# The routing stage of a fused encoder block: tiles signalled singly, bf16 counts, a shorter chain of small operations, batched one-hot tables, and a gather straight from the table

## The reference

```python
mixed = (g_attn * (attn @ w_branch_attn) + g_rnn * (rnn @ w_branch_rnn)) @ w_out
x = x + gate_m * _rmsnorm(mixed, g_post_mix)
h = _rmsnorm(x, g_pre_ffn) * (1 + scale_f) + shift_f
logits = h @ w_router + b_router
top_val, top_idx = lax.top_k(logits, 4)
top_w = softmax(top_val)
# every token goes to its 4 experts; an expert works on blocks of at most 128 rows
y[t] = sum_k top_w[t, k] * expert[top_idx[t, k]](h[t])
x = x + gate_f * _rmsnorm(y, g_post_ffn)
```

## Time and profile before

| | us |
|---|---|
| median of 3 timed runs | 1868.07 (1867.8 to 1868.69) |
| the profiled execution's own time | 1865.61 |
| its span in the profile | 1863.9 |
| PE busy in the span | 1677.9 (90%) |
| DVE, ACT, POOL busy | 1386.0, 1048.5, 303.3 |

### The profile page before, as it was taken

The page is one execution under the profiler, slowest core; times in us unless marked ns, Lnnn a source line. Parts: engine busy times, 40 slices in busy tenths (PEclk is TensorE's granted clock), DMA queues, the critical chain, the costliest instruction groups (busy, mean ns, idle before and its releaser), DMA issues.

```text
span 1863.9 us, 21055 instructions
## 1 busy us (share of the span) xinstructions
PE 1677.9 (90%) x6959; PEld 1241.7 (67%) x6959; DVE 1386.0 (74%) x1228; ACT 1048.5 (56%) x1037; POOL 303.3 (16%) x282
## 2 busy tenths in 40 slices
PE   1899999988897568999999999999999999999872
PEld 1667678876676556777767777777776777777640
DVE  5778755765553757888898898898889889888626
ACT  2246732455521315776687677677667757766511
POOL 0400000100000010231321322223142132322010
PEclk9899999998999569999999999999999999999985
DMA  8434145221136337999999999999999999999535
GB/s 316 131 136 136 51 143 202 93 72 46 46 135 224 147 142 287 392 400 392 406 407 388 389 418 384 383 412 393 378 401 399 382 378 415 380 375 404 203 143 227
DMA packets 113857, 519.83 MB, mean 279 GB/s; under 512 B 17555, under 2 KB 50675, under 8 KB 59507
## 3 DMA queue, kind: packets, MB, share of 16 engines
q1 hardware_dynamic: 98970, 491.34, 67.3%
q0 software_dynamic: 9568, 17.23, 2.7%
q10 hardware_dynamic: 5272, 10.67, 1.6%
HBM read 514.46 MB, written 19.66 MB: 287 GB/s over the span
## 4 chain that ended last, share of the span: by engine, by line
PE 63%; DVE 15%; issue 9%; ACT 8%; DMA 3%; SPq 1%; POOL 0%; DVEq 0%; POOLq 0%; ACTq 0%
PE ps L2064 28%; PE ps L2080 13%; PE ps L1797 9%; DVE lo L1649 7%; PE ps L1982 2%; PE ps L1997 2%; PE ps L2036 2%; ACT hi L1075 2%; ACT hi L846 1%; DMA xt<-x_dram 1%; PE ps L2051 1%; PE ps L1864 1%; PE ps L1911 1%; PE ps L2044 1%; DVE gmin L1682 1%
## 5 line engine op out<-in xcount | busy, mean ns | idle before, releaser
L1649 DVE TENSOR_TENSOR lo<-raw,hi 128x2048 fp32r<-128x2048 f32 x318 | 716.7, 2286 | 155.0 <-ACT hi L1075 155.0
L1075 ACT ACTIVATE hi<-raw 128x2048 fp32r<-128x2048 f32 x318 | 596.8, 1911 | 231.3 <-PE ps L2064 217.0
L1797 PE MATMUL ps<-hT,hi 128*128 128x512 f32 x720 | 240.6, 409 | 15.9 <-DVE qbd L1416 8.1
L2064 PE MATMUL ps<-hi,x_a 128*128 128x512 f32 x864 | 243.0, 411 | 0.0
L742 POOL TENSOR_TENSOR ticks<-eps 128x1 f32<-128x1 f32 x100 | 78.5, 785 | 740.6 <-ACT ysb L1112 716.2
L2064 PEld LDWEIGHTS ps<-hi,x_a 128*128 128x128 f32 x864 | 162.3, 191 | 42.3 <-issue 9.4
L1797 PEld LDWEIGHTS ps<-hT,hi 128*128 128x128 f32 x720 | 138.7, 193 | 54.6 <-issue 15.9
L1797 PE MATMUL ps<-hT,lo 128*128 128x512 f32 x360 | 142.9, 397 | 0.0
L2064 PE MATMUL ps<-hi,x_b 128*128 128x512 f32 x480 | 137.1, 407 | 3.9 <-DVE lo L1649 2.8
L2080 PE MATMUL ps<-raw,a 128*128 128x512 f32 x288 | 129.4, 592 | 0.0
L2064 PE MATMUL ps<-raw,x 128*128 128x512 f32 x288 | 129.4, 592 | 0.0
(11 more groups left out here) (325 smaller groups left out, 2510.0 us busy)
## 6 DMA issues: line engine op xcount, KB each, us to landing
raw<-w_e_dram SPq DMA_DIRECT2D x396, 1024.0 KB, 8.8
raw<-w_ada_dram SPq DMA_DIRECT2D x24, 1024.0 KB, 6.8
raw<-w_in_dram SPq DMA_DIRECT2D x15, 1024.0 KB, 5.6
raw<-w_merge_gate_dram SPq DMA_DIRECT2D x8, 1024.0 KB, 5.3
yk<-yk_d SPq DMA_DIRECT2D x4, 2048.0 KB, 14.5
raw<-w_branch_rnn_dram SPq DMA_DIRECT2D x8, 640.0 KB, 4.8
raw<-w_branch_attn_dram SPq DMA_DIRECT2D x4, 1024.0 KB, 5.0
raw<-w_out_dram SPq DMA_DIRECT2D x4, 1024.0 KB, 4.8
```

What stands on the lines that cost most here:

```text
L1075: s.activation(hi[u.slot(i)][:, :], raw[i][:, :], ACT.Copy).then_inc(hi_done, 1)
L1649: v.tensor_tensor(lo[i][:, :], raw[i][:, :], hi[u.slot(i)][:, :].bitcast(F32), ALU.subtract).then_inc(split_done, 1)
L1797: last = mm(ps[:, bank, :], wk[:, k, c0:c0 + P], acts[xa][:, k0 + k, :], start=start and k == 0 and q == 0, stop=stop and k == kn - 1 and ...
L2064: last = mm(ps[:, q, :], x_, w[:, q * 512:(q + 1) * 512], start=False, stop=i == M1 - 1, skip_group_check=True)
```

## The change

It touches the routing stage alone.

- The last matmul of each of the first three tiles now raises a semaphore of its own, `op_ps`; ACT's `post_norm` waits for its own tile, and the fourth tile keeps the old wait.
- `hfT` becomes two buffers used in turn.
- `mask` is written as bf16 (`mask16`, with a fifth block of zeros), and the counts are made by bf16 matmuls: one of 160 columns against the triangle, then 10 of 32 columns against ones; the fifth block of columns is the count. All lie in one PSUM bank.
- The chain on DVE reads ranks and counts in place, does the overflow test for ranks and counts in one instruction of 160 columns, leaves out the copy and one memset (`iota_k` is prepared beforehand), and orders independent instructions so that each second one goes without a wait. The product with `oh` is one instruction of 512 columns instead of four of 128.
- The one-hot tables are made in two halves of 8 groups with three instructions each, in the type fp32r; PE waits once for each half.
- POOL zeroes `xg` before it waits for the table (it now also waits for the transfer of `x2`), and gathers by the table's first column itself.
- Buffers move (`oh_slot`, `pairs`, `prod`), and the table gets one more column. DVE has 5 more small instructions beside the output projection.

```diff
@@ tiles
+        hfT = [z(f"hfT{i}", [P, KT, P], F32, kb) for i, kb in enumerate((88, 106))]
-        oh_slot = z("oh_slot", [P, TOPK * TT, P], F32, 64)
-        oh_blk = z("oh_blk", [P, TOPK * TT, 64], F32, 72)
+        oh_slot = z("oh_slot", [P, TOPK * TT, P], F32R, 118)
+        oh_blk = z("oh_blk", [P, TOPK * TT, 64], F32R, 72)
+        mask16 = z("mask16", [P, TT + 1, NE], BF16, 117.5)
@@ gpsimd
-            pool.wait_ge(tab_done, 1)
             for i in range(TT):
                 pool.wait_ge(h2_out[i], 16)
+            pool.wait_ge(x2_out, 16)
             g.memset(xg[:, :], 0.0).then_inc(xg_zero, 1)
             pool.wait_ge(xg_zero, 1)
+            pool.wait_ge(tab_done, 1)
...
-            g.tensor_copy(idx_now[:, 0:1], tok_i[:, 0:1]).then_inc(idx_done, 1)
-            pool.wait_ge(idx_done, 1)
-            gather_dma()
+            gather_dma(tok_i[:, 0:1])
@@ scalar
-            act.wait_ge(chunk_used, W_MIX)
...
             def post_norm(i):
+                if i < TT - 1:
+                    act.wait_ge(op_ps, i + 1)
+                else:
+                    act.wait_ge(chunk_used, W_MIX)
...
-                if i:
-                    act.wait_ge(lg_ps, i)
-                s.activation(hfT[:, :, :], ...
+                if i >= 2:
+                    act.wait_ge(lg_ps, i - 1)
+                s.activation(hfT[i % 2][:, :, :], ...
@@ vector
+            v.tensor_copy(ahead16[:, :], before[:, :])
+            v.tensor_copy(ones16[:, :], ones[:, :])
+            link(v.tensor_copy(iota_k[:, :], iota_f[:, 0:NE]))
+            v.memset(iota_k[:, 0:1], -1e6)
+            link(v.memset(mask16[:, TT, :], 0.0))
...
-            link(v.tensor_copy(cnt, ps[:, 1, 0:NE]))
-            link(v.scalar_tensor_tensor(out=key, in0=cnt, scalar=float(NE), in1=iota_e, op0=ALU.mult, op1=ALU.subtract))
-            link(v.memset(key[:, 0:1], 1e6))
+            ranks = ps[:, 0, 0:(TT + 1) * NE].rearrange("p (i e) -> p i e", e=NE)
+            rank, cnt = ranks[:, 0:TT, :], ranks[:, TT, :]
+            link(v.scalar_tensor_tensor(out=key, in0=cnt, scalar=float(NE), in1=iota_k[:, :], op0=ALU.mult, op1=ALU.subtract))
...
+            link(v.tensor_scalar(q1, q0, 0.0, None, ALU.is_ge))
+            link(v.scalar_tensor_tensor(out=q1, in0=q0, scalar=float(P), in1=q1, op0=ALU.is_ge, op1=ALU.add))
+            v.tensor_scalar(pos, pos, -1.0, 0.0, ALU.add, ALU.max)
+            link(v.scalar_tensor_tensor(out=q1, in0=q0, scalar=float(2 * P), in1=q1, op0=ALU.is_ge, op1=ALU.add))
...
-            for t, val in ((0, blk), (1, q0)):
-                for k in range(TOPK):
-                    ins = v.tensor_tensor(prod[:, TT * k:TT * k + TT, :], oh[:, TT * k:TT * k + TT, :], val, ALU.mult)
-                link(ins)
+            for t, val in ((0, blk), (1, mask)):
+                link(v.tensor_tensor(prod4, oh4, val.unsqueeze(1).to_broadcast([P, TOPK, TT, NE]), ALU.mult))
                 link(v.tensor_reduce(pick[:, t, :], prod[:, :, :], AX_X, ALU.add))
...
             dve.wait_ge(x2_out, 16)
-            for q in range(TOPK * TT):
-                v.tensor_scalar(oh_slot[:, q, :], iota_f[:, :], pick[:, 1, q:q + 1], None, ALU.is_equal)
-                v.tensor_scalar(oh_blk[:, q, 0:N_TAB], iota_f[:, 0:N_TAB], pick[:, 0, q:q + 1],
-                                asgv[:, q // TT, q % TT:q % TT + 1], ALU.is_equal, ALU.mult).then_inc(oh_done, 1)
+            half = TOPK * TT // 2
+            for q in range(0, TOPK * TT, half):
+                n = slice(q, q + half)
+                link(v.tensor_tensor(oh_blk[:, n, 0:N_TAB], iota_f[:, 0:N_TAB]..., pick[:, 0, n]..., ALU.is_equal))
+                v.tensor_tensor(oh_slot[:, n, :], iota_f[:, :]..., pick[:, 1, n]..., ALU.is_equal).then_inc(oh_done, 1)
+                v.tensor_tensor(oh_blk[:, n, 0:N_TAB], oh_blk[:, n, 0:N_TAB].bitcast(F32), asgv..., ALU.mult).then_inc(oh_done, 1)
@@ tensor
+                    if q == 3 and i < TT - 1:
+                        last.then_inc(op_ps, 1)
                 last.then_inc(chunk_used, 1)
...
-            for i in range(TT):
-                for j in range(i + 1):
-                    mm(ps[:, 0, i * NE:(i + 1) * NE], before[:, :] if j == i else ones[:, :], mask[:, j, :], ...)
-            for i in range(TT):
-                last = mm(ps[:, 1, 0:NE], ones[:, :], mask[:, i, :], start=i == 0, stop=i == TT - 1)
+            mm(ps[:, 0, 0:(TT + 1) * NE], ahead16[:, :], mask16[:, :, :]..., start=True, stop=False, ...)
+            for j in range(TT):
+                for i in range(j + 1, TT + 1):
+                    last = mm(ps[:, 0, i * NE:(i + 1) * NE], ones16[:, :], mask16[:, j, :], start=False, stop=j == TT - 1, ...)
...
             for q in range(TOPK * TT):
-                pe.wait_ge(oh_done, q + 1)
+                if q % (TOPK * TT // 2) == 0:
+                    pe.wait_ge(oh_done, 2 + 2 * (q // (TOPK * TT // 2)))
                 last = mm(ps[:, 2, 0:N_TAB], oh_slot[:, q, :], oh_blk[:, q, 0:N_TAB], start=q == 0, stop=q == TOPK * TT - 1)
```

More of the change, by code:

```diff
@@ L295, in hybrid_block @@
         freq = keep("freq", [P, 1])
+        ahead16 = keep("ahead16", [P, P], BF16)
+        ones16 = keep("ones16", [P, P], BF16)
+        iota_k = keep("iota_k", [P, NE])
         topw = keep("topw", [P, TT, TOPK])
@@ L807, in _ @@
                     b = At(NE, t)
-                    gather(b, 2, b(2, 2))
-                    scatter(b, 1, CAP_A, b(2, 3))
+                    gather(b, 2, b(2, 1))
+                    scatter(b, 1, CAP_A, b(2, 2))
                     freed(b, 1)
             b = At(NE, n_over)
-            scatter(b, 1, CAP_A, b(2, 2))
+            scatter(b, 1, CAP_A, b(2, 1))
         @block.scalar
@@ L1034, in h2_columns @@
                 act.wait_ge(h2_tr, i + 1)
-                if i:
-                    act.wait_ge(lg_ps, i)
-                s.activation(hfT[:, :, :], ps[:, 2 * i:2 * i + 2, :].rearrange("p b (k n) -> p (b k) n", n=P), ACT.Copy).then_inc(hfT_done, 1)
+                if i >= 2:
+                    act.wait_ge(lg_ps, i - 1)
+                s.activation(hfT[i % 2][:, :, :], ps[:, 2 * i:2 * i + 2, :].rearrange("p b (k n) -> p (b k) n", n=P), ACT.Copy).then_inc(hfT_done, 1)
             post_norm(0)
@@ L1501, in _ @@
             lg = route[:, 0:TT, :]
-            mask, q0, q1, blk = (route[:, 4 * t:4 * t + 4, :] for t in range(1, 5))
-            cnt, key, rk, pos, capn, exc, nb, incl, dpos = (vals[:, t, :] for t in range(9))
+            mask, blk = route[:, 4:8, :], route[:, 8:12, :]
+            q0, q1 = route[:, 12:17, :], route[:, 17:22, :]
+            key, rk, pos, capn, incl, dpos = (vals[:, t, :] for t in range(6))
             iota_e = iota_f[:, 0:NE]
@@ L1577, in _ @@
-            link(v.tensor_scalar(pos, pos, -1.0, 0.0, ALU.add, ALU.max))
-            link(v.scalar_tensor_tensor(out=exc, in0=cnt, scalar=float(-CAP_A), in1=capn, op0=ALU.add, op1=ALU.subtract))
-            link(v.tensor_scalar(nb, exc, 1.0, None, ALU.is_ge))
-            for t in range(1, 3):
-                link(v.scalar_tensor_tensor(out=nb, in0=exc, scalar=float(t * P + 1), in1=nb, op0=ALU.is_ge, op1=ALU.add))
+            v.scalar_tensor_tensor(out=q0[:, TT, :], in0=cnt, scalar=float(-CAP_A - 1), in1=capn, op0=ALU.add, op1=ALU.subtract)
@@ L1582, in _ @@
+            nb = q1[:, TT, :]
+            q0, q1 = q0[:, 0:TT, :], q1[:, 0:TT, :]
             link(v.tensor_tensor_scan(out=incl, data0=ones[:, 0:NE], data1=nb, initial=0.0, op0=ALU.mult, op1=ALU.add))
+            v.tensor_scalar(q0, q0, 0.0, None, ALU.is_ge)
             link(v.scalar_tensor_tensor(out=dpos, in0=incl, scalar=float(LAST), in1=nb, op0=ALU.add, op1=ALU.subtract))
             link(v.tensor_tensor(dpos, dpos, pos, ALU.subtract))
-            rank = ps[:, 0, 0:TT * NE].rearrange("p (i e) -> p i e", e=NE)
@@ L1587, in _ @@
-            excr = lg
-            link(v.scalar_tensor_tensor(out=excr, in0=rank, scalar=float(-CAP_A), in1=each(capn), op0=ALU.add, op1=ALU.subtract))
-            link(v.tensor_scalar(q0, excr, 0.0, None, ALU.is_ge))
-            link(v.scalar_tensor_tensor(out=q1, in0=excr, scalar=float(P), in1=q0, op0=ALU.is_ge, op1=ALU.add))
-            link(v.scalar_tensor_tensor(out=q1, in0=excr, scalar=float(2 * P), in1=q1, op0=ALU.is_ge, op1=ALU.add))
             link(v.tensor_tensor(blk, q0, each(dpos), ALU.mult))
+            v.tensor_tensor(q0, q0, each(capn), ALU.mult)
@@ new lines, in _ @@
+            for q in range(0, TOPK * TT, half):
+                n = slice(q, q + half)
+                link(v.tensor_tensor(oh_blk[:, n, 0:N_TAB], iota_f[:, 0:N_TAB].unsqueeze(1).to_broadcast([P, half, N_TAB]),
+                                     pick[:, 0, n].unsqueeze(2).to_broadcast([P, half, N_TAB]), ALU.is_equal))
+                v.tensor_tensor(oh_slot[:, n, :], iota_f[:, :].unsqueeze(1).to_broadcast([P, half, P]),
+                                pick[:, 1, n].unsqueeze(2).to_broadcast([P, half, P]), ALU.is_equal).then_inc(oh_done, 1)
```

(4 more changed lines are left out.)

46 lines of the change are left out of this document (24 added, 22 removed).

## The result

The changed kernel takes 1851.56 us, the median of 4 runs (1849.45 to 1852.5), against 1868.38 (1867.8 to 1871.15, 4 runs) for the kernel before: a ratio of 0.9904, with a 95% interval of 0.9891 to 0.9916. The forecast was 1852.4. The profiled execution took 1849.45 us, with a span of 1847.7, 16.2 shorter than that of before.

What follows compares the result with a forecast made beforehand. The prediction took a serial chain through ACT, DVE, PE, POOL and one DMA before the first expert matmul as the bound. Terms 8.2 + 1.1 + 1.3 + 2.0 + 0.7 + 2.4 = 15.7 us gave 1852.4, range 1848.0 to 1858.5.

Steps and rivals of the forecast that it cites:

- What bounds the kernel: Between output projection and first expert matmul (595.50 to 675.40 us), a serial chain bounds; a microsecond saved there shortens the end.
- Start of the norms: ACT's norms after the output projection: starting when tile 0 is complete moves the whole norm stage 8.2 us earlier.
- Second buffer: Copies into `hfT` before the last logits: with two buffers the copy lies beside tile 2's logits, saving 1.1 us.
- Counts: PE's count matmuls after the mask: bf16 saves PE 4 us, but DVE's `lo` chunks leave only 1.3 us.
- Chain: DVE's instructions from the counts to the one-hot tables: 12.06 us become 10.1, saving 2.0 us; bounds 9.5 and 11.
- Tables: One-hot tables on DVE and their PE matmuls: 7.64 us become 6.9 with one-pass fp32r, saving 0.7 us.
- Gather: POOL's gather after the table: early memset and no index copy leave 6.1 of 8.5 us, saving 2.4 us.
- fp32r in two passes: Rival at PE's table matmuls: two passes each, so the stage loses 2.3 us instead of winning 0.7; 1855.4 us; chance 0.12.
- Early signal without effect: Rival at ACT's norm start: ACT or DVE is held elsewhere, so 8.2 us less gain; 1860.6 us; chance 0.04.
- Slow gather from the strided column: Rival at POOL's gather: building addresses from indices 200 bytes apart costs more; 1878 us at 0.2 us per index; chance 0.03.
- The late transfer: Rival at the last `modulate`: the first `h2` buffer's transfer lands late, losing 5.2 us; 1857.6 us; chance 0.06.
- The clock that stays up: Rival in transposes and logits: PE keeps 2.4 GHz, so some 6 us more go; 1846.4 us; chance 0.05.

Runs made afterwards that it cites:

- the fillers: The changed kernel with 47 extra bf16 matmuls of 512 columns, results unused, spread among PE's transposes and logits before the experts; 1847.02 us.

## Why the prediction was right, step by step

**What bounds the kernel.** Right: 15.73 us less at the first expert's bias matmul (675.40 to 659.67) became 16.2 in the span and 16.8 in the medians. The experts give nothing back and take nothing, within the us or so that they vary.

**Start of the norms, 8.2.** Measured 8.2 against the projection's end in the two profiles, and 8.17 by undoing it. The profile of the changed kernel shows it as 7.3, since its projection ended 0.9 later. The slack was there: DVE's preparation ended at 585.8, tile 0 at 588.3.

**Second buffer, 1.1.** 1.64, and 1.66 by undoing it: the term furthest off in us. "I count nothing for it", said of DVE's wait before the last `modulate`, was worth 0.24. The other miss is a reading: the prediction lets the last logits start where the chain shows those of tile 2 ended, at 627.85, while groups back to back start 3.26 us apart, which is 0.2 earlier.

**Counts, 1.3.** 1.42, and for the reason given: DVE's `lo` chunks. PE was far faster than I took it to be: 11 bf16 passes in 0.58 us, where I had 2.4 from the float32 pitch. It changed nothing here, as the cover of 4.2 us took it all, and it decides what the next step is worth: 4.2 us by moving two instructions.

**Chain, 2.0.** From the key to the first one-hot instruction: 631.50 to 641.45, 9.95 instead of 12.06, so 2.11. The prediction's pieces add up to 10.0 and not to its 10.1.

**Tables, 0.7.** 641.45 to 648.00, 6.55 instead of 7.66: 1.11. One pass for fp32r was right, and shown by the float32 tables (+2.94). DVE's two halves took 4.55 for 4.5; what follows them took 2.00 for 2.4, so the 0.6 that I had estimated for latency and signal was too much.

**Gather, 2.4.** 2.17 by the step, 2.16 in the profile (9.48 to 7.32 from the table read to the landing), 2.28 by undoing it. The copy's 1.16 did not pass to the gather, nor to POOL's next copy, which took 0.18. DVE was ready 1.66 before ACT, where 1.4 was forecast.

**The rivals.** fp32r in two passes: shown wrong. Early signal without effect: shown wrong. Slow gather from the strided column: shown wrong, 2.25 us against 2.28. The late transfer did not occur: DVE went into the last `modulate` without a wait. But it was nearer than the prediction had it. Its bound of 7.9 us came from transfers of `h2` that started later, and in the changed kernel the four took longer (L1040):

```profile
DMA to landing us min/median/max: 8.5/10.1/13.9
```

The first, the one that counts, took 8.7 of the 11.3 us that it had; with the third one's 13.9 it would have been late. POOL's memset of `xg` did wait for the last one, until 625.34, some 24 us before the table. (The 18.3 us of the earlier trace rows are the longest of the experts' weight chunks, not of the trace: the load of `xt` took 19.5. Nothing hangs on it here.) The clock that stays up did not come by itself, and its price was too high: some 6 us were forecast, and with the fillers that made it true 4.61 were won. That 1847.02 lies so near the 1846.4 of that rival is chance, as the changed kernel was itself 0.8 below its forecast. The Trainium skill (TensorE: Matmul & The Clock Gate, "Part 4: PE-mode transpose") says that transposes don't count as PE being busy in the same way; these runs agree as far as they go (0.50 from 606 to 617 us, where PE did nothing but transposes and logits and was busy for 10.91 of 11 us). No stretch here has transposes alone, and with fillers around them they did run at 1.00. Of float32 passes of 32 columns the section says nothing; logits alone kept PE busy from 617.0 to 623.7 without a gap, and the granted clock stayed at 0.50.

The sum was 15.7, and the terms measured in the two profiles make 8.2 + 1.6 + 1.4 + 2.1 + 1.1 + 2.2 = 16.6 against the projection's end, 0.9 of which were lost ahead of it in the profiled execution. So the mechanism of each term is right, and most were somewhat low: four by 0.1 to 0.5 us, the gather's 0.2 too high. The near hit of 15.73 on 15.7, and of 659.67 on the forecast 659.7, is luck: those 0.9 us cancelled what the terms had too little.

## What to carry to other kernels

When a step waits for the later of two engines, price both: the bf16 counts saved PE 4.4 us and the kernel 0.2, until two instructions of the other engine were moved into its own waits. A gain on a serial chain ahead of a bound stretch was worth its full length here, so such a chain is the first place to look in a kernel whose PE is 90% busy.
